# A hybrid attention layer on one core: head norms by a product with ones, and two changes of order

## What is computed

```python
h = rmsnorm(x, norm_w[layer]);  proj = h @ w_in[layer]
# proj: q, k, v of 8 stick-breaking heads, q, k, v of 8 forgetting heads, 8 forget logits,
#       q of 4 memory heads, and a gate of width 20*64
z = q @ k.T * scale                                  # stick-breaking, s < t strictly
a = exp(log_sigmoid(z) + suffix_sum(-softplus(z)))
p = softmax(q @ k.T * scale + logf[t] - logf[s])     # forgetting, s <= t
p = softmax(q @ mem_k.T * scale)                     # memory, 256 tokens
y = concat(heads)                                    # 20 heads of 64
yf = y * rsqrt(mean(y * y, per head of 64) + EPS) * out_norm_w
x = x + (yf * silu(gate)) @ w_out[layer];  out = rmsnorm(x, final_norm_w)
```

## Time and profile before

| | before |
|---|---|
| median of 3 runs | 866.95 us (865.5 to 867.22) |
| the profiled execution's own time | 867.22 us |
| its span in the profile | 865.5 us |
| PE busy | 822.7 us, 95% |
| PE's weight loads busy | 685.4 us, 79% |
| DVE busy | 582.8 us, 67% |
| ACT busy | 479.5 us, 55% |
| POOL busy | 250.1 us, 29% |

### The profile page before, as it was taken

How to read it: one execution, slowest core, us unless ns; L and a number is a source line. 1 busy time by engine, 2 the same in 40 slices (tenths; PEclk the granted TensorE clock), 3 DMA queues, 4 the chain that set the end, 5 groups by cost and what they waited for, 6 DMA issues and landing times.

```text
span 865.5 us, 12331 instructions
## 1 busy us (share of the span) xinstructions
PE 822.7 (95%) x4304; PEld 685.4 (79%) x4304; DVE 582.8 (67%) x1203; ACT 479.5 (55%) x932; POOL 250.1 (29%) x377
## 2 busy tenths in 40 slices
PE   8998988899999999999999999999999997999996
PEld 7667766788888878888878888878887886878885
DVE  5744545556767787775788785778766676775575
ACT  5744657675576555667555567655555683542231
POOL 1133543433124522422354231344323111420000
PEclk9999999999999999999999999999999999999999
DMA  7023793320300320030313104020301298152432
GB/s 294 25 70 120 276 301 136 147 96 26 98 25 30 93 98 26 25 98 25 86 36 98 38 13 122 25 74 25 122 25 48 76 337 288 55 170 73 171 122 97
DMA packets 33372, 88.94 MB, mean 103 GB/s; under 512 B 3352, under 2 KB 11544, under 8 KB 32288
## 3 DMA queue, kind: packets, MB, share of 16 engines
q1 hardware_dynamic: 28992, 72.44, 25.8%
q10 hardware_dynamic: 4320, 15.73, 4.8%
HBM read 57.72 MB, written 21.53 MB: 92 GB/s over the span
## 4 chain that ended last, share of the span: by engine, by line
PE 75%; DVE 10%; ACT 6%; issue 3%; DMA 3%; POOL 2%; ACTq 0%; SPq 0%; DVEq 0%; POOLq 0%
PE banks L645 13%; PE banks L647 12%; PE banks L646 12%; PE banks L687 9%; PE banks L801 7%; PE banks L819 4%; PE banks L818 4%; PE banks L787 4%; PE banks L788 4%; DVE work L1426 2%; PE banks L839 2%; DMA wo_dram<-work 1%; DVE pT L1463 1%; DVE work L1429 1%; POOL w_parts L1203 1%
## 5 line engine op out<-in xcount | busy, mean ns | idle before, releaser
L645 PE MATMUL banks<-hT,w_parts 128*128 128x512 f32 x576 | 242.3, 421 | 9.1 <-DVE fx_heads L1356 3.7
L646 PE MATMUL banks<-hT,w_parts 128*128 128x512 f32 x576 | 227.1, 394 | 0.0
L647 PE MATMUL banks<-hT,w_parts 128*128 128x512 f32 x576 | 227.1, 394 | 0.0
L1463 DVE TENSOR_TENSOR pT<-banks,pT 128x512 fp32r<-128x512 f32 x208 | 112.0, 564 | 127.1 <-ACT pT L999 126.4
L999 ACT ACTIVATE pT<-banks 128x512 fp32r<-128x512 f32 x208 | 97.2, 499 | 177.7 <-PE banks L801 176.9
L1203 POOL TENSOR_TENSOR w_parts<-w_raw,w_parts 128x1024 fp32r<-128x1024 f32 x40 | 96.3, 2407 | 133.8 <-ACT w_parts L913 133.8
L645 PEld LDWEIGHTS banks<-hT,w_parts 128*128 128x128 f32 x576 | 109.4, 190 | 26.0 <-DVE fx_heads L1356 4.4
L647 PEld LDWEIGHTS banks<-hT,w_parts 128*128 128x128 f32 x576 | 109.1, 189 | 24.7
L646 PEld LDWEIGHTS banks<-hT,w_parts 128*128 128x128 f32 x576 | 109.9, 191 | 12.8
L1426 DVE TENSOR_TENSOR_SCAN work<-work 128x639 f32<-128x639 f32 (+3 forms) x64 | 91.7, 1433 | 6.9 <-POOL work L1211 6.4
L801 PE MATMUL banks<-ident,work 128*128 128x128 f32 x640 | 95.3, 276 | 0.0
(11 more groups left out here) (209 smaller groups left out, 1382.1 us busy)
## 6 DMA issues: line engine op xcount, KB each, us to landing
w_raw<-in_w_tiles SPq DMA_DIRECT2D x40, 512.0 KB, 3.3
wo_dram<-work ACTq DMA_DIRECT2D x16, 512.0 KB, 3.7
hT<-wo_dram SPq DMA_DIRECT2D x16, 512.0 KB, 8.1
work<-in_w_out ACTq DMA_DIRECT2D x8, 512.0 KB, 4.1
fx_heads<-fx_heads SPq DMA_DIRECT2D x8, 512.0 KB, 8.4
negL<-negL_dram SPq DMA_DIRECT2D x8, 512.0 KB, 7.3
yT_dram<-silu SPq DMA_DIRECT2D x8, 512.0 KB, 5.0
sb_heads<-sb_heads SPq DMA_DIRECT2D x8, 512.0 KB, 7.4
```

The source lines that it names most:

```text
L645: pe.matmul(o, w[:, 0, k, :], hT[:, 0, k, tok], start=(k == 0), stop=False)
L646: pe.matmul(o, w[:, 0, k, :], hT[:, 1, k, tok], start=False, stop=False)
L647: mm = pe.matmul(o, w[:, 1, k, :], hT[:, 0, k, tok], start=False, stop=(k == KT - 1))
L1463: dve.tensor_tensor(pT[:, n % 3, 1, cols], banks[:, T_BANK + n % 2, cols], pT[:, n % 3, 0, cols].bitcast(F32), ALU.subtract).then_inc(t_lo, 1)
```

## The change

Three things change.

1. **Head norms.** ACT squares a half of yT (128 rows of head dimensions by 512 tokens) into `o_tmp`, one tick earlier than before (`square_half`, ticks 2 and 6), as soon as DVE has written that half. PE's N1 piece then multiplies each of the four 128x128 blocks of squares (as the stationary operand) by `pair_ones`, 128x2, which has ones in rows 0 to 63 of column 0 and rows 64 to 127 of column 1. The sums over each head's 64 dimensions come out as 8 columns, and DVE reads them from PSUM without a reduction. `pair_ones` is filled by four memsets of DVE at the start. `output_lo`, which also writes `o_tmp`, waits for the N1 piece where it has to.
2. **Order on ACT and DVE.** In a tick with a small piece, ACT and DVE now do their work on it before that on the transposed P.
3. **Diagonals.** POOL makes `diag` for a unit in that unit's tick, no longer one tick ahead.

```diff
-                    pe.wait_ge(o_read, 4 * p.of + 2 + TURN[p.c] + 1)
+                    pe.wait_ge(sq_done, 2 * p.of + TURN[p.c] + 1)
+                    pe.wait_ge(ones_done, 1)
                     for b in range(4):
-                        t = 4 * p.c + b
-                        mm = pe.transpose(o[:, b * P:(b + 1) * P], yT[:, t * P:(t + 1) * P], ident[:, :])
+                        mm = pe.matmul(o[:, 2 * b:2 * b + 2], o_tmp[:, b * P:(b + 1) * P], pair_ones[:, :], start=True, stop=True)
...
+                if t.h == 0 and t.c == 1 and t.ph:
+                    act.wait_ge(small_ready, small_of("N1", 0, t.ph - 1) + 1)
+                if t.h == 1 and t.c == 0:
+                    act.wait_ge(small_ready, small_of("N1", 1, t.ph) + 1)
                 act.activation(o_tmp[other, :], banks[other, O_BANK, :], ACT.Copy).then_inc(o_lo, 1)
 
-            def square_rows(n):
-
-                act.wait_ge(small_ready, n + 1)
-                act.activation(banks[:, SMALL_BANK, :], banks[:, SMALL_BANK, :], ACT.Square).then_inc(sq_done, 1)
+            def square_half(g):
+                t = UNIT[4 * g]
+                act.wait_ge(o_read, g + 1)
+                act.activation(o_tmp[:, :], yT[:, t.c * CW:(t.c + 1) * CW], ACT.Square).then_inc(sq_done, 1)
...
+                if i - 1 in OUT_AT and OUT_AT[i - 1] % 4 >= 2:
+                    square_half(OUT_AT[i - 1])
                 for q in READ[i]:
                     evacuate(q)
                     split_next(q)
-                for n in T_AT[i]:
-                    upper_part(n)
                 for n in SMALL_AT[i]:
                     if SMALL[n].what == "VT":
                         values_hi(n)
-                    if SMALL[n].what == "N1":
-                        square_rows(n)
                     if SMALL[n].what == "N3" and SMALL[n].of >= LAST - 1:
                         y_end_hi(SMALL[n].of - LAST + 1, SMALL[n].c)
+                for n in T_AT[i]:
+                    upper_part(n)
...
                 if i < N_UNITS and UNIT[i].kind == "sb":
                     masks(i)
-
-                if i + 1 < N_UNITS and UNIT[i + 1].kind == "fx":
-                    diagonal(i + 1)
+                elif i < N_UNITS and UNIT[i].kind == "fx":
+                    diagonal(i)
...
-                    dve.wait_ge(sq_done, 2 * p.of + TURN[p.c] + 1)
+                    dve.wait_ge(small_ready, n + 1)
                     mine = slice(NB * p.c, NB * (p.c + 1))
-                    half, sums = head3[:, 2, mine], head_sums[:, mine]
-                    link(dve.reduce_sum(sums, src.rearrange("p (n d) -> p n d", d=HD), AX_X))
+                    half = head3[:, 2, mine]
                     if PHASES[p.of][0] == "sb":
-                        ins = dve.tensor_scalar(half, sums, 1.0 / HD, EPS, ALU.mult, ALU.add)
+                        ins = dve.tensor_scalar(half, src[:, 0:NB], 1.0 / HD, EPS, ALU.mult, ALU.add)
...
+            dve.memset(pair_ones[0:HD, 0:1], 1.0)
+            dve.memset(pair_ones[0:HD, 1:2], 0.0)
+            dve.memset(pair_ones[HD:P, 0:1], 0.0)
+            dve.memset(pair_ones[HD:P, 1:2], 1.0).then_inc(ones_done, 1)
...
-                for n in T_AT[i]:
-                    lower_part(n)
                 for n in SMALL_AT[i]:
                     finish_small(n)
                     if SMALL[n].what == "N3" and SMALL[n].of >= LAST - 1:
                         y_end_lo(SMALL[n].of - LAST + 1, SMALL[n].c)
+                for n in T_AT[i]:
+                    lower_part(n)
```

More of the change, by code:

```diff
@@ L321, in hybrid_layer @@
         ident = sb("ident", [P, P])
+        pair_ones = sb("pair_ones", [P, 2])
         out_g = sb("out_g", [P, NT_OUT])
@@ L330, in hybrid_layer @@
         head3 = sb("head3", [P, 3, 2 * NB])
-        head_sums = sb("head_sums", [P, 2 * NB])
         x_sums = sb("x_sums", [P, NB + MB])
@@ L421, in hybrid_layer @@
         row_in = [sem(f"row_in{b}") for b in range(NB + MB)]
-        ident_zero, ident_done = sem("ident_zero"), sem("ident_done")
+        ident_zero, ident_done, ones_done = sem("ident_zero"), sem("ident_done"), sem("ones_done")
         x_ssq, x_ssq_dve, x_r, x_scaled, x_scaled_act = sem("x_ssq"), sem("x_ssq_dve"), sem("x_r"), sem("x_scaled"), sem("x_scaled_act")
@@ L1402, in finish_small @@
                         link(dve.scalar_tensor_tensor(out=half, in0=total, scalar=EPS, in1=total, op0=ALU.mult, op1=ALU.mult))
-                        ins = dve.scalar_tensor_tensor(out=half, in0=sums, scalar=1.0 / HD, in1=half, op0=ALU.mult, op1=ALU.add)
+                        ins = dve.scalar_tensor_tensor(out=half, in0=src[:, 0:NB], scalar=1.0 / HD, in1=half, op0=ALU.mult, op1=ALU.add)
                     ins.then_inc(small_done, 1)
```

## The result

The changed kernel takes 878.89 us (median of 4 runs, 877.83 to 881.8) against 866.28 us for the kernel before beside it (865.5 to 867.22). The ratio is 1.0157, 95% interval 1.0133 to 1.0182: slower by 12.6 us. The profiled execution of the changed kernel took 882.52 us with a span of 880.8, 15.3 us more than the profiled one of before. That is more than the medians differ by: over all 21 executions of the changed kernel that were timed the times go from 876.28 to 882.52 us with a median of 880.75, and the profiled one is the slowest of them.

What follows compares the result with a forecast made beforehand. PE was taken to bound most of phases 2 to 9, DVE and ACT mattering only where PE waits. Terms 5.0 + 1.8 + 3.5 + 2.9 + 1.0 + 0.4 = 14.6 us, on 865.5 + 1.7, gave 881.8, rounded to 882 us; range 871 to 888.

Steps and rivals of the forecast that it cites:

- rival (f): DVE's 0.685 us reductions, not PE, hold up the end: 12.3 us less, 855 us; chance 6%.
- Part 1, 0.45 us for an N1 step: Head norms on PE: new products take 0.90 us a step, 0.45 more than the transposes; 5.0 us in all.
- (b): Two-column products cost 0.055 us a record, so the N1 step costs PE nothing more: 875 us; chance 17%.
- (d): Weight loads in the N1 step do not overlap: 1.1 instead of 0.45 us a step, 891 us; chance 6%.
- Four passes with a load each: N1 step on PE, if float32 needed a load per pass: 1.8 us a step, total about 13 us beyond forecast.
- Tick 3 of phases 3, 5 and 7: Without DVE's reduction the scan starts some 0.7 us earlier and PE's waits of 0.8 to 1.1 go: -1.35 us.
- Part 2, the late diagonal: Diagonal behind POOL's row_scales and splits: PE waits 0.9 us in phases 4 and 6, 2.8 and 2.6 in 2 and 8.
- What tick 10 gives back: Phases 2 and 8: PE's later waits of 0.9 and 1.0 us for the output rows go, leaving 3.5 us net.
- The clock: A clock drop behind each of PE's two long waits, phases 2 and 8, 1.45 us of work each: 2.9 us.
- Part 3, the order: Swapped order on ACT and DVE: the V piece of tick 6 costs PE 0.3 + 0.2 us in phases 4 and 6: 1.0.
- The late ticks: Ticks 10 and 11 of phases 4 and 6, with the late diagonal: 0.2 us each, 0.4 in all.
- Phases 0, 1 and 9: N1 steps there: 0 in phase 1, hidden by PE's waits; 0.45 us in phase 9 and 0.9 in the tail.

Runs made afterwards that it cites:

- e5: Kernel before with only the new head norms, their squares and block of ones in float32r instead of float32: 863.19 us, ratio 0.9971.
- e6: Kernel before with only the new float32 head norms, each of the four products done twice, the second into unread columns: 882.26 us, ratio 1.0183.
- e8: Kernel before with new head norms in float32r and, on DVE, the head-norm piece ahead of the P part: 860.43 us, ratio 0.9931.
- e4: Kernel before with only the swapped order on ACT and DVE, small piece ahead of the transposed P: 873.53 us, ratio 1.0079.
- e11: Kernel before with only the old head-norm pieces put ahead of the P part on ACT and DVE: 870.68 us, ratio 1.0061.
- e9: e8 with the square of the row sums (the operation on 8 columns) done by ACT instead of DVE: 857.9 us, ratio 0.9916.
- e1: Changed kernel with the diagonals made one tick ahead again, head norms and order still changed: 870.81 us, ratio 1.0045.
- e7: Changed kernel with POOL's weight split moved behind the next diagonal in phases 2 and 8: 873.84 us, ratio 1.009.
- e3: Kernel before with only the diagonals changed, each made in its own unit's tick: 882.92 us, ratio 1.0186.
- e10: Kernel before with only the values and output pieces put ahead of the P part on ACT and DVE: 867.96 us, ratio 1.0025.

## Why the prediction came out

Forecast 882 us, range 871 to 888, slower with 0.86. Measured 878.9, slower.

**What bounds the kernel** held in the main: where PE has no wait, DVE's lighter load pays nothing. But the forecast looked for places where it does pay only in tick 3 of phases 3, 5 and 7, and e5 shows two others, tick 10 of phases 2 and 8, where the reduction gone shortens PE's path by 0.6 to 0.7 us. In all the lighter load is worth 3.3 us (e5), not the 12.3 of rival (f).

**Part 1, 0.45 us for an N1 step,** measured 0.46 in ticks 3 and 7 of phases 2 to 8. The reading of the load spacing from the warm-up and the score pair was right (0.111 us), and rivals (b) and (d) fell with it. e5 and e6 show that the number of records is the cause: halved, the cost is 0, doubled, it is 0.89 more. The Trainium skill (TensorE: Matmul & The Clock Gate, "Back-to-back issue gap") gives about 25 ns for an isolated product of 1 to 64 columns and says that this leaves out the weight loads. Here each product brings its own 128x128 load, the records are 0.111 us apart, and the figure, which the forecast quoted without that condition, doesn't apply. Four passes with a load each, as the forecast worked out from the Trainium skill (FP8 and Floating Point Precision, "TensorE Precision Notes"), would have made the step 1.8 us; the records are two a product, and the eight took 0.97 us.

**Tick 3 of phases 3, 5 and 7** was the step that failed. I took the scan's start to hang on DVE's reduction, so that without it the waits of 0.8, 0.8 and 1.1 us would vanish: -1.35 in all. They went from 2.6 to 1.9 us only. These phases grew by 2.0 where I had 0.0. The rows of the changed kernel in phase 5:

```profile
418.44 2.38 POOL L1207 TENSOR_TENSOR w_parts<-w_raw,w_parts 128x1024 fp32r<-128x1024 f32 x1 [0.90 <-ACT w_parts L913]
419.31 1.54 DVE L1404 SCALAR_TENSOR_TENSOR head<-rowsum 128x8 f32<-128x8 f32 x1 [1.16 <-PE banks L753]
...
421.29 2.28 DVE L1428 TENSOR_TENSOR_SCAN work<-work 128x1023 f32<-128x1023 f32 x1
```

and of the kernel before:

```profile
409.53 2.40 POOL L1203 TENSOR_TENSOR w_parts<-w_raw,w_parts 128x1024 fp32r<-128x1024 f32 x1 [0.91 <-ACT w_parts L913]
...
411.38 0.57 DVE L1402 SCALAR_TENSOR_TENSOR head<-rowsum 128x8 f32<-128x8 f32 x1
```

Before, the split ended at 411.93, the 8-column operation at 411.95, and the scan began at 412.07, 0.14 us behind the split. POOL set the scan's start, not the reduction; the reduction, which reads PSUM, ran beside the split for nothing. In the changed kernel the scan starts 0.47 us behind the split, since the lower part of P comes after it. So the path through DVE is 0.33 later, PE is 0.46 later, and tick 5 shrinks by 0.13 (measured 0.15). The same account gives e8's +0.33 (0.31), e4's and e11's +0.33 (0.33), e5's 0 (-0.03) and e9's 2.13 - 2.42 = -0.29 (-0.28); these are the values of phases 3 and 5, and in e4 and e11 phase 7 has the same. e9 tests the account, since there the stop moved to the scan when the 8-column operation was gone; no run moved the split itself in these phases.

**Part 2, the late diagonal.** Phases 4 and 6: 0.9 each, measured 0.85. Phases 2 and 8: waits of 2.8 and 2.6, growth of tick 8 2.64 and 2.46. e1 and e7 show the cause, POOL's queue. What tick 10 gives back was sized too low, 0.9 and 1.0 against 1.52 and 1.56 (and e1 has it without the late diagonals). I had read one wait of 0.91 us; the load row beside it in the trace of before says 1.35, and there was a second wait ahead of it:

```profile
214.90 0.19 PEld L787 LDWEIGHTS banks<-fx_heads 128*128 128x128 f32 x1 [0.49 <-DVE peak L1443]
...
217.82 0.19 PEld L818 LDWEIGHTS banks<-pT,fx_heads 128*128 128x128 f32 x1 [1.35 <-DVE yT L1472]
217.82 0.50 PE L818 MATMUL banks<-pT,fx_heads 128*128 128x512 f32 x1 [0.91 <-DVE yT L1472]
```

**The clock,** 1.45 us behind each of the two waits: tick 9 grew by 1.48 and 1.56, and in e7, without the waits, not at all. So the drops go with the waits. But a wait of that length doesn't always bring one, and the forecast took it that it does. In e3 equal waits of 2.51 us had a drop behind one and none behind the other, and PE's wait of 1.87 us for DVE's negL in phase 9 was followed by a granted clock of 1.00 in the kernel before (733 to 737 us) and of 0.57 in the changed one (748 to 752 us). What decides it is open, and that both drops came as forecast is in part luck.

**Part 3, the order.** The values piece 0.5 in each of phases 4 and 6: 0.57 (e1, e10). The late ticks 0.2 each phase: tick 12, 0.39; it is 0.0 in e1, so it belongs to the diagonals. What the order costs beside the old norms (6.9 us in e4) the forecast did not cover.

**Phases 0, 1 and 9** I had at 0 and 1.35; the trace has 1.8 and -1.0. Phase 0 alone grew by 2.5 in the changed kernel, by 0.3 to 3.6 us in ten of the eleven experiments and by -1.8 in the eleventh, in no order that follows the edits. So the one trace of before was probably quick there. In phase 9 and the tail it was probably slow, since that column is negative in every row but the forecast's and e6's, even in e3, which has no edit in phase 9. Neither was tested, and what the change itself does in these phases stays open. The sum of the forecast's terms for phases 2 to 8 is 13.2, and the trace has 14.5; the medians differ by 12.6. The surplus of the profiled executions is the changed kernel's: its profiled one lies 3.6 us above the median, that of before 0.9 above its own. Its 21 executions differ in the clock, too: the seven fastest were granted 0.988 or 0.989 over the whole span, the others, but for one, 0.984 to 0.987. That fits drops that come in some executions only, but there is no second trace of the changed kernel that shows it. The total is closer than its parts: 1.4 too much in phases 2 and 8 stands against 2.0 too little in phases 3, 5 and 7 and 0.6 in phases 4 and 6.

## What to carry over

Count records, not columns, when a product moves to PE: a float32 product with its own 128x128 weights is two loads at 0.11 us each, a float32r one is one, and on this kernel that made the same algebra 3.0 us slower or 3.3 us faster. Before crediting a lighter engine, look at what else ends at the moment it is supposed to start earlier; here it was another engine's instruction, 0.02 us away in the trace of before. An instruction moved in a queue must be priced with everything that is now ahead of it: a 2.4 us split ahead of a 0.3 us diagonal, in two phases, cost two waits of PE and two clock drops, 5 us in all (e7).

## What the runs showed of the hardware

A DVE operation with both inputs in SBUF doesn't run beside POOL's elementwise operation on SBUF: the one that comes later stands until the other has ended. Twelve traces have the operation on 8 columns beside POOL's split in phases 3, 5 and 7, 36 times in all; it took 0.56 to 2.00 us according to how early it came and ended 0.02 to 0.03 us behind POOL's every time; DVE operations with one input in PSUM kept their length. It also goes the other way: in e8 POOL's mask at 407.69 took 1.56 us instead of 0.29 and ended at 409.25, behind DVE's scan (409.16). The Trainium skill (SBUF — State Buffer, "SBUF: two separate sides") states this: the two engines share a port pair, a DVE operation with two SBUF inputs needs it against a GpSimd operation that reads SBUF, and whichever starts first holds it for its whole instruction. The traces agree; I had not weighed it in the forecast. The profile counts the standing time as busy time, with no wait in brackets, so it shows only as an odd length of a small operation.
